# Two gram products side by side in one pair of banks, and one mask for both heads, in the recurrence of a fused two-block kernel

## What is computed

```python
w = jnp.exp(-DECAY_SCALE * jax.nn.sigmoid(w_logit))
kk = kk / jnp.maximum(jnp.linalg.norm(kk, axis=-1, keepdims=True), 1e-12)
def step(S, inp):
    r_t, w_t, k_t, v_t, kk_t, a_t = inp
    sa = jnp.einsum('bhvk,bhk->bhv', S, -kk_t)
    S = S * w_t[:, :, None, :] + sa[..., None] * (kk_t * a_t)[:, :, None, :] \
        + v_t[..., None] * k_t[:, :, None, :]
    return S, jnp.einsum('bhvk,bhk->bhv', S, r_t)
_, y = lax.scan(step, S0, (r, w, k, v, kk, a))
# then y is centred and scaled for each head, a bonus is added, and it is gated
```

## Time and profile before

| | us |
|---|---|
| median of 3 runs | 1963.77 (1962.88 to 1965.16) |
| the profiled execution | 1962.61 |
| its span | 1960.8 |
| TensorE busy | 1864.6 |
| VectorE busy | 959.2 |
| ACT busy | 804.7 |
| GpSimd busy | 412.1 |

### The profile page before, as it was taken

One profiled execution on the slowest core, in us unless ns is written; L12 is line 12 of the kernel. 1 busy time (PEld: TensorE's weight loads), 2 busy tenths in 40 slices (PEclk: granted clock), 3 DMA queues, 4 the chain that ended last, 5 costly groups with the idle time before them and its releaser, 6 DMA issues.

```text
span 1960.8 us, 39071 instructions
## 1 busy us (share of the span) xinstructions
PE 1864.6 (95%) x16241; PEld 1525.1 (78%) x16241; DVE 959.2 (49%) x2200; ACT 804.7 (41%) x1805; POOL 412.1 (21%) x416
## 2 busy tenths in 40 slices
PE   6999999999997999989999999999999999999998
PEld 6997766888885999767777777777777686667898
DVE  5677766143335153046554444444444456774523
ACT  5346666244345143233333333333333256554421
POOL 4550000212114332223222222222222111001221
PEclk9999999999998999999999999999999999999999
DMA  5152300423431412421112211211122220005432
GB/s 183 45 181 78 85 25 1 134 77 113 138 100 44 172 66 85 120 83 58 58 58 64 74 58 58 61 58 58 58 66 66 74 80 34 2 1 172 156 134 87
DMA packets 148855, 159.93 MB, mean 82 GB/s; under 512 B 14948, under 2 KB 132008, under 8 KB 148680
## 3 DMA queue, kind: packets, MB, share of 16 engines
q1 hardware_dynamic: 148456, 156.44, 25.1%
q0 software_dynamic: 224, 0.99, 0.2%
HBM read 110.53 MB, written 52.62 MB: 83 GB/s over the span
## 4 chain that ended last, share of the span: by engine, by line
PE 81%; DVE 7%; ACT 4%; DMA 3%; issue 2%; POOL 2%; SPq 0%; DVEq 0%; POOLq 0%; ACTq 0%
PE ps L679 9%; PE ps L680 8%; PE ps L681 8%; PE ps L951 8%; PE ps L953 7%; PE ps L952 7%; PE ps L1054 5%; PE ps L789 3%; PE ps L768 3%; PE ps L1091 3%; PE ps L776 3%; PE ps L1238 2%; PE ps L1120 2%; DMA t<-in_w_in 2%; PE ps L1261 2%
## 5 line engine op out<-in xcount | busy, mean ns | idle before, releaser
L679 PE MATMUL ps<-t,t 128*128 128x256 f32 (+2 forms) x1392 | 433.6, 311 | 9.1 <-DVE t L2137 4.2
L2719 POOL TENSOR_TENSOR t<-t,t 128x512 fp32r<-128x512 f32 x183 | 237.7, 1313 | 917.7 <-ACT t L1337 893.0
L680 PE MATMUL ps<-t,t 128*128 128x256 f32 (+2 forms) x1392 | 426.7, 307 | 0.0
L681 PE MATMUL ps<-t,t 128*128 128x256 f32 (+2 forms) x1392 | 426.5, 306 | 0.0
L951 PE MATMUL ps<-t,t 128*128 128x512 f32 (+2 forms) x720 | 298.4, 414 | 0.9 <-ACT t L1613 0.9
L679 PEld LDWEIGHTS ps<-t,t 128*128 128x128 f32 x1392 | 268.1, 193 | 27.1 <-issue 13.7
L681 PEld LDWEIGHTS ps<-t,t 128*128 128x128 f32 x1392 | 267.9, 192 | 10.7
L680 PEld LDWEIGHTS ps<-t,t 128*128 128x128 f32 x1392 | 268.1, 193 | 10.3 <-issue 0.2
L953 PE MATMUL ps<-t,t 128*128 128x512 f32 (+2 forms) x720 | 268.9, 373 | 0.0
L952 PE MATMUL ps<-t,t 128*128 128x512 f32 (+2 forms) x720 | 268.5, 373 | 0.0
L1337 ACT ACTIVATE t<-t 128x512 fp32r<-128x512 f32 x182 | 107.9, 623 | 144.2 <-DMA t<-in_w_in 88.5
(11 more groups left out here) (269 smaller groups left out, 2988.7 us busy)
## 6 DMA issues: line engine op xcount, KB each, us to landing
t<-in_w_in SPq DMA_DIRECT2D x53, 512.0 KB, 6.0
zgate_spill<-t SPq DMA_DIRECT2D x20, 512.0 KB, 3.2
tile_bias<-t SPq DMA_DIRECT2D x16, 576.0 KB
t<-tile_bias SPq DMA_DIRECT2D x8, 1152.0 KB, 6.1
t<-in_x SPq DMA_DIRECT2D x16, 512.0 KB, 9.1
t<-zgate_spill SPq DMA_DIRECT2D x16, 512.0 KB, 3.6
feat_spill<-t SPq DMA_DIRECT2D x13, 512.0 KB, 3.2
tile_bias<-band_bias SPq DMA_DIRECT2D x48, 128.0 KB
```

The source lines that it names most:

```text
L679: e.matmul(dst, lh, rh, start=k == 0, stop=False)
L680: e.matmul(dst, lh, rl, start=False, stop=False)
L681: m = e.matmul(dst, ll, rh, start=False, stop=k == n - 1)
L2719: e.tensor_tensor(WLO[wslot(b)][:, o], WST[:, o], WHI[wslot(b)][:, o].bitcast(F), ALU.subtract).then_inc(w_lo.sem, w_lo.up((b, p)))
```

## The change

Three things are changed, all in the recurrence.

The transposed gram is made first and gram 0 after it, in the same two banks, which lie side by side: the transposed gram from column 256, gram 0 from column 0. A new function `mine_two` takes two adjacent banks of the slot's three, and both are held until one event. `psum_two` gives a view over both banks. One mask operation of 256 columns (two heads) now stands for two of 128, for all three grams. The same holds for the plan's four products: each has two adjacent banks and one operation that empties both.

The order of the masks is now `ND`, `NDT`, `ARB`, `NOT`, then gram 1's. The waits that named the second half of an operation name the one operation. Since a pair always takes banks 0 and 1 or 1 and 2 of the slot's three, each pair that follows a pair shares at least one bank with it.

The sum of the chain (`YT`) is issued before the last chain step's `yield`, not after it.

```diff
+        def psum_two(key, first, width):
+            lower = where.get(key(0), 0)
+            return ps_all[:, :].rearrange("p (b c) -> p b c", c=512)[:, lower:lower + 2, first:first + width]
...
+                def mine_two(key, emptied):
+                    slot_turn[n] += 2 + (slot_turn[n] % 3 == 1)
+                    return [bank_at((u, (key, x)), 3 * n + slot_turn[n] % 3 - 1 + x, emptied) for x in range(2)]
...
-                def grams(key, width, left, right, done):
-                    ps = [mine((key, x), (gram_v, (u, done, x))) for x in range(2)]
+                def grams(key, ps, c0, width, left, right):
...
-                            i = e.matmul(ps[x][64 * q:64 * q + 64, width * m:width * m + width], left(pr, 2 * m + q), right(pr, 2 * m + q), start=True, stop=True)
+                            o = slice(c0 + width * m, c0 + width * m + width)
+                            i = e.matmul(ps[x][64 * q:64 * q + 64, o], left(pr, 2 * m + q), right(pr, 2 * m + q), start=True, stop=True)
...
-                for s, done in ((0, "arb"), (1, "rkt")):
-                    grams(s, 128, lambda pr, c: BK[pr, c, s, :], lambda pr, c: AR[pr, :, c, :], done)
+                for s, done in ((0, "not"), (1, "rkt")):
+                    ps = mine_two(("gram", s), (gram_v, (u, done)))
                     if s == 0:
-                        grams("t", 64, lambda pr, c: AR[pr, 0, c, :], lambda pr, c: BK[pr, c, 0, :], "not")
+                        grams("t", ps, 256, 64, lambda pr, c: AR[pr, 0, c, :], lambda pr, c: BK[pr, c, 0, :])
+                    grams(s, ps, 0, 128, lambda pr, c: BK[pr, c, s, :], lambda pr, c: AR[pr, :, c, :])
                     yield INV_US
...
-                w.wait_ge(*gram_v[u, "not", 1])
+                w.wait_ge(*gram_v[u, "ndt"])
...
-                    ps = [mine((name, q), (emptier, (u, name, q))) for q in range(2)]
+                    ps = mine_two(name, (emptier, (u, name)))
...
+                def gram(key, side, dst, k, name):
+                    w.wait_ge(*gram_mm[u, key])
+                    c0, width = (256, 64) if side is None else (0, 128)
+                    pv = psum_two(lambda x: (u, (("gram", key), x)), c0, MP * width).rearrange("p x (m c) -> p x m c", c=width)
+                    if side is not None:
+                        pv = pv[:, :, :, 64 * side:64 * side + 64]
+                    e.tensor_tensor(dst[:, :, :].rearrange("p (x m) c -> p x m c", x=2), pv, bc(mask(k, MP), 1, 2), ALU.mult).then_inc(gram_v.sem, gram_v.up((u, name)))
+
+                gram(0, 0, ND, C_MD, "nd")
+                gram(0, None, NDT, C_MDT, "ndt")
+                gram(0, 1, ARB, C_MI, "arb")
+                gram(0, None, NOT, C_MOT, "not")
+                yield INV_US
+                gram(1, 0, AKT, C_MS, "akt")
+                gram(1, 1, RKT, C_MI, "rkt")
+                yield INV_US
...
                     if c == CU_ - 1:
                         il.units += 1
+                        w.wait_ge(*chain_mm[u, "y", CU_ - 1])
+                        w.wait_ge(*plan_a[u, "y"])
+                        if before >= 0:
+                            w.wait_ge(*d_y[n][before])
+                        e.tensor_tensor(YT[:, :], psum((u, "yb"))[:, 0:TU], S.YL[:, :, :].rearrange("p c t -> p (c t)"), ALU.add).then_inc(
+                            chain_v.sem, chain_v.up((u, "y")))
                     yield CHAIN_US
-                w.wait_ge(*chain_mm[u, "y", CU_ - 1])
...
```

More of the change, by code:

```diff
@@ L1063, in unit @@
                 yield INV_US
-                w.wait_ge(*gram_v[u, "rkt", 1])
+                w.wait_ge(*gram_v[u, "rkt"])
                 w.wait_ge(*prep_a[u, "turn", "v"])
@@ L1092, in full @@
                     i.then_inc(inv_mm.sem, inv_mm.up((u, key)))
+                w.wait_ge(*gram_v[u, "not"])
                 w.wait_ge(*inv_v[u, "d4", 1])
@@ L1136, in unit @@
                         w.wait_ge(*prep_p[u, "state"])
-                    w.wait_ge(*plan_v[u, "q", 1])
+                    w.wait_ge(*plan_v[u, "q"])
                     if not (h == 3 and c == CU_ - 1):
@@ L1627, in unit @@
                     w.wait_ge(*norm2_v[before, "gated"])
-                    w.wait_ge(*plan_a[before, "y", 1])
-                    w.wait_ge(*plan_v[before, "q", 1])
+                    w.wait_ge(*plan_a[before, "y"])
+                    w.wait_ge(*plan_v[before, "q"])
                     w.wait_ge(*chain_mm[before, "y", CU_ - 1])
@@ L1704, in unit @@
                         w.wait_ge(*plan_mm[u, name])
[L1705 to L1708, removed]
+                        pv = psum_two(lambda q: (u, (name, q)), 0, 64 * MP).rearrange("p q (m c) -> p q m c", c=64)
+                        e.activation(dst[:, :, :].rearrange("p (m q) c -> p q m c", q=2), pv, ACT.Copy).then_inc(plan_a.sem, plan_a.up((u, name)))
                     yield INV_US
@@ L2438, in unit @@
                         w.wait_ge(*plan_mm[u, name])
[L2439 to L2446, removed]
+                        pv = psum_two(lambda q: (u, (name, q)), 0, 64 * MP).rearrange("p q (m c) -> p q m c", c=64)
+                        dst, other = (S.MTS[:, :, :], DG[:, :, :]) if name == "mt" else (S.QSS[:, :, :], AR[:, 1])
+                        dst, other = (b_.rearrange("p (m q) c -> p q m c", q=2) for b_ in (dst, other))
+                        e.tensor_tensor(dst, pv, other, ALU.add).then_inc(plan_v.sem, plan_v.up((u, name)))
                     yield INV_US
@@ L2454, in unit @@
                         w.wait_ge(*chain_mm[u, "state", c])
-                        w.wait_ge(*plan_a[u, "g", 1])
+                        w.wait_ge(*plan_a[u, "g"])
                         if c:
@@ L2463, in unit @@
                         il.units += 1
-                    yield CHAIN_US
-                w.wait_ge(*chain_mm[u, "y", CU_ - 1])
[L2466 to L2470, removed]
+                        w.wait_ge(*chain_mm[u, "y", CU_ - 1])
[4 more added lines that the diff above has]
+                            chain_v.sem, chain_v.up((u, "y")))
+                    yield CHAIN_US
                 def normal(key):
@@ L2904, in unit @@
                 yield INV_US
-                w.wait_ge(*gram_v[u, "nd", 1])
+                w.wait_ge(*gram_v[u, "nd"])
                 w.wait_ge(*prep_v[u, "bonus"])
```

## The result

The changed kernel takes **1937.16 us** (median of 4 runs, 1936.42 to 1938.99) against 1963.33 for the kernel before, measured beside it (1959.32 to 1965.16): ratio 0.9871, 95% interval 0.9854 to 0.9888. The prediction had 1946.0 and a range down to 1939. The direction and the mechanisms were right.

A forecast was written before the change was run, and what follows sets the result against it. TensorE, busy 95% of the span, was taken as the bound. 9.3 + 7.8 + 1.5 - 0.5 - 0.3 = 17.8 us off 1962.61 gave 1944.8, with the median 1.16 above: 1946.0 us, range 1939 to 1954.

The forecast's parts named there:

- What bounds the kernel: Whole kernel: TensorE, busy 95% of the span; only what makes it stand still counts, waits of 13.3 and 8.8 us.
- Rival 3: After the touched places: freed time is stopped further on; half lost gives 1955 (6%), nearly all 1962 (4%).
- The gram step: First gram product to gram 1: 0.21 us gained in 6 units, 0.89 in 9, together 9.3 us.
- the release: Gram step: gram 1 can start 0.15 us after the fourth mask ends, at 2.77 after the step's start.
- The masks: Gram step: four operations of 256 columns, 0.42 us each, starting 0.34 apart, nothing added for crossing banks.
- Rival 5: Gram step: masks over two banks may cost 0.69 us, one every 0.69; slower, 1971 us; 4% with milder forms.
- rival 2: Gram step: masks run one after the other, 3.6 us lost, 1949.6 us; 8%.
- The new wait in place of the old: Gram step with one k-step: gram 1 newly waits 0.68 us for the masks, in 6 units.
- The centring product: Odd units: the earlier sum removes TensorE's wait, 0.97 us in each of 8 places, 7.8 us.
- The last unit: Last centring product, whose sum stands behind sixteen scalings: 1.5 us gained, bounds 0 and 1.83.
- Plan and n2t: Plan products wait for whole operations, -0.5 us; n2t waits for the last gram 1 mask in one unit, -0.3.
- The base: Starting time: profiled execution 1962.61 us, with the median of the runs 1.16 above it.

The follow-up runs named there:

- e5: The changed kernel with each merged mask cut into two operations of one head each: median 1944.3 us, ratio 0.9904 to the kernel before.
- e12: The changed kernel with the chain's last sum back at its old place, behind the step's end: median 1948.6 us, ratio 0.9931.
- e6: The kernel before with only the plan's four evictions merged, one operation for two banks: median 1961.5 us, ratio 0.9999.
- e3: The changed kernel with the plan's four evictions as they were, two operations each: median 1941.4 us, ratio 0.9892 to the kernel before.

## Why the prediction was right or wrong, point by point

- **What bounds the kernel: right.** TensorE's two waits were the change's whole worth, 21.4 us of 22.1 at one clock. Nothing came back after 1561 us: from the last k-step on, the traces of the changed kernel are 0.1 to 2.3 us shorter. Rival 3 (freed time stopped further on) shows only as waits of 0.7 to 1.2 us that come and go between executions.
- **The gram step: the mechanism right, the term mis-sized, 9.3 predicted and 12.1 measured.** This is the step that failed. Two of its parts were off. First, the transposed gram was priced at 0.34 us, half of the 0.68 of the plan's 32 products. It holds TensorE 0.23: the chain product follows the step's first product by 936.93 - 936.21 = 0.72, of which gram 0 is 0.49. The rows had it all along: in the earlier trace rows the transposed gram starts at 941.79 and the chain product behind it at 942.04, 0.25. That starts the masks 1.07 us after the step's first product instead of 1.18, 0.11 in the 6 units with one k-step, and brings gram 1 after 2.64 instead of 2.78, 0.14 in the 9 with two: 1.9 us. Second, the release (from the end of the last mask to the product that waits for it) was priced at 0.15, taken from the earlier trace rows; the last mask ends at 937.28 + 1.42 = 938.70 and gram 1 starts at 938.75, 0.05 later, and e5 shows about the same (940.75 + 1.68 = 942.43, start 942.48). It was 0.05 in 5 of the 6 units that wait and 0.15 in the other, so 0.5 us; why it differs is open. Third, not foreseen, one step with two k-steps (986.54 in the trace of before) had waited 1.17 us for the mask where its like wait 0.81, 0.4 us more. Together they are about the 2.8.
- **The masks: right.** Four start 0.33 apart (3 x 0.33 + 0.42 = 1.41, and the row has 1.42) and none costs more for reading across two banks, which the prediction had argued from a reduction and not from such a mask. Rival 5, priced at 0.69 each, is out, and so is rival 2: one after the other they would take 4 x 0.416 = 1.66. The page of the Trainium skill on which rival 2 leaned ("VectorE: DVE Perf Modes", section "The DRAIN you can't avoid") adds in the same paragraph that a next operation that is not held starts earlier. With that sentence it was no rule against the change, and the row agrees with it.
- **The new wait in place of the old: right in kind**, in the 6 units with one k-step and the first; 0.47 us on average (2.8 in 6, in the row of e12) where 0.68 was predicted, from the same two parts.
- **The centring product: right.** 7.8 predicted for 8 places; 7.5 measured, 0.92 to 0.99 each. **The last unit:** 1.5 predicted, 1.82 measured, its upper bound: the wait of L978 behind it (0.21 in the earlier trace rows) is 0.21 in the changed kernel too, so nothing was late next.
- **Plan and n2t: -0.8 predicted.** For the plan the runs give -0.4 (e6, uncertainty 0.5) to +1.3 (e3, 0.8), so no loss is shown. n2t waits for its mask once, 0.2 us, in the traces of the changed kernel (L1065 for L2402), close to the 0.3. In the intervals the two are lost among the others. So 0.8 of the 3.6 us between 17.8 and 21.4 are these terms, and 2.8 the gram step.
- **The base.** The mis-sized terms alone would not have put the result outside the range: with 21.4 us in place of 17.8 the forecast would have been 1942.4. The other 5.2 us to 1937.2 are mostly the two sets of runs that were compared. The sum started from the median of three runs, 1963.8, where all runs of before give 1961.4 at a clock of 0.994: 2.4 us. The changed kernel's four runs had a mean clock of 0.9948, and all 13 of its runs give 1939.4 at 0.994: 2.2 us, of which the clock is 1.0. The last 0.6 is within the uncertainty. The profiled execution of before, on whose trace the terms were read, had itself 1.7 us in its first 36 from the clock, and its span is 3.1 above the second one's.
- **The range** was too narrow for that: it took its ends from the terms of the change alone and left nothing for the spread of the runs on both sides, 1.4 to 2.1 us each.

## What to carry to other kernels

Where two products wait for evictions in turn, put all products of the step ahead of the first eviction, on shared banks: here that gave 8.6 of 12.1 us, and merging the evictions 3.5. An operation that a critical product needs belongs into the stream of its engine where its operands are ready, ahead of whatever waits for something later; moving one sum of 0.42 us gave 9.3 us. Price short products by the difference of two starts around just such products, not as a share of a longer group; and before explaining the last two or three microseconds, take a second trace of the unchanged kernel and compare the granted clock stretch by stretch.

## What the runs showed of the hardware

- One VectorE operation that reads 128 columns in each of two neighbouring banks takes 0.42 us, as one of 256 columns in one bank does, and two such start 0.33 apart.
- Gram 1 started 0.05 us after the end of the last mask in five of its seven waits and 0.15 after it in the first two, in all three traces of the changed kernel, and with masks of 128 columns (e5) likewise. In both traces of before, the transposed gram started 0.15 after its mask in all 16 units. What decides it is open.
- The granted clock of TensorE fell to its lower level for a few microseconds in some executions and not in others, at places with the same work: 0.95 over the first 36 us in one of two executions of the kernel before, and 0.95 from 1480 to 1515 us in one of three of the changed kernel. What decides it was not tried.
